# A ring of fourteen weight chunks, stripes of 1024 and transposes by VectorE in the expert stage of a decoder trunk

## The reference

```python
def swiglu(h, w1, w3, w2):
    return (jax.nn.silu(h @ w1) * (h @ w3)) @ w2

def moe_ffn(h, router_w, w1, w3, w2):      # h (256, 1024); w1, w3 (8, 1024, 3584); w2 (8, 3584, 1024)
    logits = (h @ router_w).astype(jnp.float32)
    vals, idx = lax.top_k(logits, 2)
    probs = jax.nn.softmax(vals, axis=-1)
    gate = jnp.sum(jax.nn.one_hot(idx, 8) * probs[..., None], axis=-2)
    out = jnp.zeros_like(h)
    for e in range(8):
        out = out + gate[..., e:e + 1] * swiglu(h, w1[e], w3[e], w2[e])
    return out
```

## Time and profile before

| | us |
|---|---|
| median of 3 runs (lowest, highest) | 1647.84 (1646.87, 1651.17) |
| the profiled execution, its own time | 1651.2 |
| its span, first to last instruction | 1649.4 |
| TensorE busy | 1614.8 (98%) |
| VectorE, ScalarE, GpSimd busy | 582.3, 397.8, 404.5 |
| mean granted TensorE clock | 0.99 |
| read from memory | 472 MB, 290 GB/s over the span |

### The profile page before, as it was taken

How to read it: one execution, slowest core, us unless ns; L and a number is a source line. 1 busy time by engine, 2 the same in 40 slices (tenths; PEclk the granted TensorE clock), 3 DMA queues, 4 the chain that set the end, 5 groups by cost and what they waited for, 6 DMA issues and landing times.

```text
span 1649.4 us, 46626 instructions
## 1 busy us (share of the span) xinstructions
PE 1614.8 (98%) x20940; PEld 1498.3 (91%) x20940; DVE 582.3 (35%) x784; ACT 397.8 (24%) x527; POOL 404.5 (25%) x541
## 2 busy tenths in 40 slices
PE   8999999999999999999999999999999999999998
PEld 5887888999978788899999999999999999999997
DVE  4799866466568977510000000000000000000002
ACT  4245455544454554510000000000000000000000
POOL 8856900999434523120000000000000000000100
PEclk9899999999999999999999999999999999999999
DMA  8453456556544455389999999999999999999996
GB/s 298 130 177 128 145 176 229 186 195 206 179 154 129 147 173 178 120 293 374 392 387 387 390 391 387 387 387 393 389 387 395 385 389 392 389 386 391 395 394 255
DMA packets 212094, 481.10 MB, mean 292 GB/s; under 512 B 7936, under 2 KB 32640, under 8 KB 211696
## 3 DMA queue, kind: packets, MB, share of 16 engines
q1 hardware_dynamic: 207456, 463.34, 77.4%
q0 software_dynamic: 4064, 14.95, 2.7%
q10 hardware_dynamic: 432, 0.65, 0.1%
HBM read 472.49 MB, written 6.42 MB: 290 GB/s over the span
## 4 chain that ended last, share of the span: by engine, by line
PE 67%; DVE 2%; DMA 1%; ACT 0%; issue 0%; DVEq 0%
PE ps L1336 33%; PE ps L1333 20%; PE ps L676 2%; PE ps L677 2%; PE ps L678 2%; PE ps L1364 2%; DMA raw<-moe_w 1%; PE ps L722 1%; PE ps L723 1%; PE ps L724 1%; DVE w_lo L306 1%; PE ps L912 0%; PE ps L1425 0%; PE ps L1300 0%; PE ps L1406 0%; DVE keybias L2169 0%
## 5 line engine op out<-in xcount | busy, mean ns | idle before, releaser
L1336 PE MATMUL ps<-raw,xgT 128*32 128x128 f32 x5424 | 611.6, 273 | 0.0
L1333 PE MATMUL ps<-raw,xgT 128*32 128x384 f32 x5424 | 604.2, 487 | 1.6 <-DMA raw<-moe_w 1.6
L1336 PEld LDWEIGHTS ps<-raw,xgT 128*32 128x32 f32 x5424 | 587.5, 110 | 0.0
L1336 PE MATMUL ps<-raw,hidT 128*32 128x128 f32 x2640 | 297.5, 273 | 0.0
L1333 PE MATMUL ps<-raw,hidT 128*32 128x384 f32 x2640 | 293.9, 486 | 0.0
L1336 PEld LDWEIGHTS ps<-raw,hidT 128*32 128x32 f32 x2640 | 287.5, 110 | 0.0
L306 DVE TENSOR_TENSOR w_lo<-raw,w_hi 128x2048 fp32r<-128x2048 f32 (+1 forms) x97 | 238.3, 2465 | 114.2 <-ACT w_hi L300 113.6
L2591 DVE COPY hidT<-ps 128x384 f32<-128x384 f32 x55 | 30.7, 558 | 564.1 <-PE ps L1364 564.1
L300 ACT ACTIVATE w_hi<-raw 128x2048 fp32r<-128x2048 f32 (+1 forms) x97 | 185.2, 1910 | 174.9 <-PE ps L678 83.4
L1333 PEld LDWEIGHTS ps<-raw,xgT 128*32 128x32 f32 x5424 | 215.9, 109 | 10.1 <-issue 9.8
L1886 ACT ACTIVATE sil<-ps 128x384 f32<-128x384 f32 (+1 forms) x67 | 33.9, 506 | 736.9 <-PE ps L1336 736.9
(11 more groups left out here) (417 smaller groups left out, 2253.1 us busy)
## 6 DMA issues: line engine op xcount, KB each, us to landing
raw<-moe_w SPq DMA_DIRECT2D x336, 1024.0 KB, 9.8
raw<-w_in SPq DMA_DIRECT2D x44, 1024.0 KB, 5.6
raw<-ffn_w SPq DMA_DIRECT2D x33, 1024.0 KB, 5.3
raw<-w_o SPq DMA_DIRECT2D x8, 1024.0 KB, 4.9
raw<-w_out_a SPq DMA_DIRECT2D x4, 1024.0 KB, 4.8
raw<-w_out_c SPq DMA_DIRECT2D x4, 1024.0 KB, 5.0
raw<-w_out_b SPq DMA_DIRECT2D x4, 1024.0 KB, 4.9
raw<-w_in SPq DMA_DIRECT2D x4, 904.0 KB, 4.8
```

The costliest lines, as they stand in the source:

```text
L1333: pe.matmul(ps[tile_rows(g), bank, 0:WIDE], x_of(g), w[:, 0:WIDE], start=first, stop=last, skip_group_check=True, tile_position=(0, TILE * g))
L1336: mm = pe.matmul(ps[SLOTS:P, bank, g * P:(g + 1) * P], x_of(g), w[:, WIDE:HALF], start=first and g == 0, stop=last, skip_group_check=True, ...
```

## The change

- Ring of 14 chunks. The six buffers of `raw` are joined by six over `w_hi` and `w_lo` (`ring_w`) and two over `hT_hi` and `hT_lo` (`ring_h`). The first six are loaded as before, the next six when all mixer chunks are consumed, the last two when the first gather is done.
- Stripes of 1024: an expert is now three pairs of 512 channels and one single (`HALVES = (2, 2, 2, 1)`). Banks 0 and 1 take a pair's w1 product, 2 and 3 its w3 product, 4 and 5 the down sums; SiLU and multiply work on both banks at once.
- Up chunks of a pair are two row tiles of 1024 columns (runs of 4 KB). Those of the single keep four of 512. Down chunks take rows so that partition p has four rows lying together in memory, of which a chunk takes two: runs of 8 KB, every 16 KB. The hidden channels are turned in the matching order.
- No transposes on TensorE in the first round: VectorE turns `hid_pair` and the gathered tokens in blocks of 32 by 32, from SBUF to SBUF.
- Down products are split 388 + 3 x 124 columns in place of 384 + 3 x 128.
- The loops over stripes are written out; for TensorE, VectorE, ScalarE and SP an expert is one body. The first expert's loads stand ahead of SP's loop. The four stores of the output share one semaphore.

```diff
+TOKEN_AT = HALF - 32
+Y_WIDE = WIDE + 4
+Y_REST = HALF - Y_WIDE
+PAIR = 2 * HALF
+HALVES = (2, 2, 2, 1)
+RING = 14
...
+        with ExitStack() as ring:
+            ring_w = sb("ring_w", [P, 2 * SPLIT, CHUNK], F32, ring)
...
+            w2e = moe_w2[0].rearrange("e (k p j) n -> p (e k) j n", p=P, j=4)
-            w2e = moe_w2[0].rearrange("e (k p) n -> p (e k) n", p=P)
...
+                def load_ring(m, turns, src):
+                    first = rnd == 0 and isinstance(turns, int) and turns == 0 and m - MOE0 < RING
+                    if first and m - MOE0 >= RAW + 2 * SPLIT:
+                        sp.wait_ge(S["gather_ps"], 2)
+                    if first and m - MOE0 < RAW:
+                        sp.wait_ge(used, m - RAW + 1)
+                    elif first:
+                        sp.wait_ge(used, MOE0)
+                    else:
+                        sp.wait_ge(used, value(sp, m - RING + 1 + RING * turns))
+                    sp.dma_start(ring_view(m, tuple(src.shape[1:])), src).then_inc(ring_sem(m), 16)
...
                 def up(m, turns, w, e, t):
+                    ks = 4 // HALVES[t]
+                    for c in range(KD // ks):
+                        row = value(sp, KD * e + ks * c)
+                        load_ring(m + c, turns, w[:, bass.ds(row, ks), t * PAIR:t * PAIR + HALVES[t] * HALF])
                 def down(m, turns, e, t):
+                    for c in range(2 * HALVES[t]):
+                        row = value(sp, K2 * e + 2 * t + c // 2)
+                        j = 2 * (c % 2)
+                        load_ring(m + c, turns, w2e[:, bass.ds(row, 1), j:j + 2, :].rearrange("p o j n -> p (o j) n"))
...
+                def four_tiles(bank, x_of, w, first, last, wide=WIDE):
+                    rest = HALF - wide
                     for g in range(TILES):
+                        pe.matmul(ps[tile_rows(g), bank, 0:wide], x_of(g), w[:, 0:wide], start=first, stop=last,
                                   skip_group_check=True, tile_position=(0, TILE * g))
                     for g in range(TILES):
+                        mm = pe.matmul(ps[SLOTS:P, bank, g * rest:(g + 1) * rest], x_of(g), w[:, wide:HALF],
...
-                def turn_hidden(i):
-                    pe.wait_ge(S["hid_done"], i + 1)
-                    for k in range(TILES):
-                        tr = pe.transpose(ps[:, 4, k * P:k * P + P], hid[:, k * P:k * P + P], ident[:, :])
-                    tr.then_inc(S["hidT_ps"], 1)
...
+                def turn_gathered(e, w3_used):
+                    dve.wait_ge(S["xg_loaded"], value(dve, 16 * e))
+                    dve.wait_ge(used, value(dve, w3_used))
+                    for g in range(TILES):
+                        for q in range(4):
+                            src = xg_tok[tile_rows(g), :].rearrange("s (k q n) -> s k q n", k=KD, q=4)[:, :, q, :]
+                            ins = dve.transpose(xgT[tile_rows(q), :, tile_rows(g)], src)
+                    ins.then_inc(S["xg_turned"], 1)
+
+                def turn_hidden(at, halves, free, dst=hidT):
+                    dve.wait_ge(S["hid_done"], value(dve, at))
+                    if free is not None:
+                        dve.wait_ge(used, value(dve, free))
+                    turned = dst[:, 0:4 * halves * SLOTS].rearrange("p (c s) -> p c s", s=SLOTS)
+                    for h in range(halves):
+                        for g in range(TILES):
+                            for q in range(4):
+                                rows = tile_rows(g if q < TILES else TILES)
+                                col = h * WIDE + P * (q if q < TILES else g)
+                                src = hid_pair[rows, col:col + P].rearrange("s (n j) -> s j n", j=4)
+                                ins = dve.transpose(turned[tile_rows(q), 4 * h:4 * h + 4, tile_rows(g)], src)
+                    ins.then_inc(S["hidT_made"], 1)
...
+                    stripe(i + 1, n, n + 8, 2, 2)
+                        pick_slots(value(dve, e + 1), rnd)
+                    stripe(i + 2, n + 12, n + 20, 2, 2)
+                        tokens(e + 1)
+                    stripe(i + 3, n + 24, n + 28, 2, 1)
+                        turn_gathered(e + 1, n + 28)
+                    stripe(i + 4, n + 32, n + 40, 1, 2)
...
-                pool.wait_ge(S["gather_ps"], 2 * e)
+                if e >= 2:
+                    pool.wait_ge(S["xg_turned"], e - 1)
```

More of the change, by code:

```diff
@@ L632, in expert @@
                 def expert(e, last):
[L633 to L641, removed]
@@ L649, in experts @@
+                    if not last:
+                        up(m, turns, w1e, e + 1, 0)
+                        up(m + 4, turns, w3e, e + 1, 0)
+                        m += 8
+                    down(m, turns, e, LAST)
+                up(n, 0, w1e, 0, 0)
+                up(n + 4, 0, w3e, 0, 0)
+                first = 0
+                if rnd == 0:
+                    expert(0, False)
+                    first = 1
+                with sp.Fori(first, EXPERTS - 1) as e:
                     expert(e, False)
@@ L1367, in down @@
-                def down(n, i, turns, first=False, middle=None):
-                    pe.wait_ge(S["hidT_copied"], i - DENSE_STRIPES)
-                    for chunk in range(2):
+                        for k in range(ks):
+                            kk = ks * c + k
+                            w = ring_view(m, (ks, HALF * halves))[:, k, :]
+                            for half in range(halves):
+                                mm = four_tiles(2 * which + half, lambda g: xgT[:, kk, tile_rows(g)],
+                                                w[:, half * HALF:(half + 1) * HALF], kk == 0, kk == KD - 1)
@@ L1371, in down @@
+                        mm.then_inc(used, 1)
+                def down(n, i, turns, halves, first=False):
+                    pe.wait_ge(S["hidT_made"], i - DENSE_STRIPES)
+                    for chunk in range(2 * halves):
                         m = n + chunk
                         loaded(m, turns)
+                        turned = hidT[:, chunk // 2 * WIDE:(chunk // 2 + 1) * WIDE]
                         for k in range(2):
                             for half in range(2):
-                                mm = four_tiles(2 + half, hidden_tile(hidT, 2 * chunk + k),
-                                                slot_view(raw, m, (2, D))[:, k, half * HALF:(half + 1) * HALF],
-                                                first and chunk == 0 and k == 0, False)
@@ L1470, in expert @@
                         pe.wait_ge(S["acc_done"], acc_before(rnd, e))
-                    down(n0 + 8, i + 1, turns, first=True)
-                    if last or rnd > 0:
+                    down(n + 8, i + 1, turns, 2, first=True)
+                    if pick_turned:
                         turn_pick(e)
-                    first = 2
-                    if rnd == 0 and not last:
-                        first = 3
-                        step(i + 1, turns + 1, middle=lambda: find_tokens(e + 1))
-                        down(n0 + 8, i + 2, turns + 1)
@@ L1479, in expert @@
-                    with pe.Fori(first, MOE_STRIPES - 1) as t:
-                        step(i + t - 1, turns + t - 1)
-                        down(n0 + 8, i + t, turns + t - 1)
-                    t = MOE_STRIPES - 1
-                    def next_tokens():
-                        if not last and rnd == 0:
-                            turn_gathered(e + 1)
-                        elif not last:
-                            pe.wait_ge(S["pickT_done"], scattered_before(rnd, e) + 1)
-                            gather(e + 1)
@@ L1493, in expert @@
-                    step(i + t - 1, turns + t - 1, after=next_tokens)
-                    down(n0 + 8, i + t, turns + t - 1, middle=(lambda: turn_hidden(i + t)) if last else None)
+                    n += 12
+                    step(n, i + 1, turns, 2)
+                    if not pick_turned:
+                        find_tokens(e + 1)
+                    down(n + 8, i + 2, turns, 2)
+                    n += 12
+                    step(n, i + 2, turns, 1)
+                    if not last and rnd > 0:
+                        pe.wait_ge(S["pickT_done"], scattered_before(rnd, e) + 1)
+                        gather(e + 1)
```

286 lines of the change are left out of this document (147 added, 139 removed).

## The result

The kernel after takes 1610.35 us (median; 1608.24 to 1611.76) against 1647.9 us before: ratio 0.9768 [0.9748, 0.9787], 37.5 us less. The forecast was 1602, some 46 us less. The profiled execution took 1608.24 us with a span of 1606.5; before it was 1651.2 and 1649.4.

A forecast was written before the change was run, and what follows sets the result against it. TensorE's fourth column group paced the passes, with DMA very near. TensorE's savings of 52.6 us gave 1587.4, the stream 1588 to 1594; last pass 1591, 49 us earlier, made 1602 us; range 1592 to 1624, 65% for 1596 to 1610.

The forecast's parts named there:

- TensorE's part: Expert stage: transposes gone, down split with drifting column groups, no stall; 52.6 us saved, last pass ending at 1587.4 us.
- the meeting of the two limits: End of expert stage: DMA and TensorE finishing together cost a little more than either; last pass taken at 1591 us.
- the pass-by-pass 109.8: Rival, expert passes: column groups cannot drift, each pass costs the slower, 109.83 us an expert; time 1606 to 1608; 7%.
- A regular wait of the down products for VectorE: Sign, once an expert: down products waiting on VectorE would show its transposes to be too slow.
- the transposes are too slow: Rival, VectorE: above 0.43 us each, every expert waits; 1615 us at 0.50, 1720 at 0.91; 5%.
- VectorE's part: Transposes of hidden pair and gathered tokens: 0.30 us per 128 columns, 7.1 us a pair, all hidden behind products.
- My limit of 0.43: VectorE's transposes before the half pair: hidden while one costs under 10.4 / 24 = 0.43 us.
- DMA's part: Expert weight stream: longer runs at 404 to 413 GB/s; last chunk lands at 1584 us, last pass 1588 to 1594.
- layout rival: Down chunk loads: 8 KB reads at 16 KB steps hit the same memory channels; decisive from 0.41 us more a chunk; 3%.
- DMA rival: Expert weight stream: long runs bring nothing, all chunks at 387 GB/s, last pass 1628, time 1639 us; 20%.
- the gathers as a lump: Last expert: 2 MB of gathers come as a lump, named beside the meeting limits in taking 1591 us.
- the waits come late: Sign of being right, expert stage: TensorE's waits for chunks are few and late.

The follow-up runs named there:

- r1: Kernel after with each down chunk loading only half its data, all engine work kept: 1600.98 us, 0.9739 of the kernel before.
- r2: r1 with the down products split evenly, 384 + 3 x 128 columns: 1606.52 us, 0.9772 of the kernel before.
- m2: Kernel after with VectorE's transposes reading contiguous columns, the multiply writing them in that order: 1610.97 us, 0.9786 of the kernel before.
- f3: f1 with the pairs' up chunks read in 2 KB runs: 1626.53 us, 0.9880 of the kernel before.
- f1: Kernel after with about half of the experts' products left out on TensorE, transfers untouched: 1600.61 us, 0.9727 of the kernel before.
- f2: f1 with down chunks of two rows lying end to end, 4 KB runs instead of 8 KB: 1605.17 us, 0.9756 of the kernel before.
- m4: Kernel after with the edits of m2 and m3 together: 1611.95 us, 0.9788 of the kernel before.
- s2: s1 with the later experts' indirect token gathers replaced by direct loads, 32 bytes a row after the second expert: 1602.86 us, 0.9742 of the kernel before.
- s1: Kernel after with the half pair's up chunks loaded in 4 KB runs, same bytes, half of them wrong columns: 1604.79 us, 0.9761 of the kernel before.
- m1: The kernel after run again unchanged, as reference on another chip: 1611.29 us, 0.9784 of the kernel before.
- m3: Kernel after with SP issuing a chunk only when the chunk six back has landed, ring still 14: 1609.91 us, 0.9779 of the kernel before.

## Why the prediction was right, and where it was short

**The number.** 1610.35 us lies inside the stated range, just past the upper end of the likely stretch (1596 to 1610). The total is closer than its terms. In the profiled execution the stage is 12.9 us longer than forecast (889.5 against 1591 - 714.41 = 876.6), and 6.2 us of that came back because the stage started sooner. Nothing in the prediction foresaw this; it is luck. Of the 12.9 us, 6.8 belong to TensorE's part (r1's 879.8 against 873.0) and 6.1 to the meeting of the two limits.

**TensorE's part: right in its mechanism, some 7 us short.** The L1364 and L1425 sets are gone. The up passes keep their times and the down passes go at 0.326 and 0.318 us; the column groups drift and the period is the larger sum, 108.9, not the pass-by-pass 109.8: r1 against r2 shows 0.80 of the 1.12 us, the rest going with the shorter wait for VectorE. To 108.9 come 0.43 us for the token search (I had 0.25) and 0.5 to 0.6 us of wait for VectorE (I had none): 109.94, which is r1's beat. Counted over the stage that is 8 x 109.94 - 0.43 = 879.1 us (879.8 in r1's trace) against my 873.0 (1587.4 - 714.41). A regular wait of the down products for VectorE, once an expert, was on my list of signs that the transposes are too slow; it was there, at 0.5 us.

**VectorE's part: mis-sized at 0.30 us, measured 0.42.** My limit of 0.43 was the cover of 10.4 us divided by 24. The 24 real ones fill 10.3 us, and TensorE still waits 0.5 us behind them, so the cover was thinner than the arithmetic said. What I had left out is the source step of four elements. m2 shows that this did not reach the time.

**DMA's part: right by itself.** 4 KB and 8 KB runs bring what the sum said, or more: f3 shows 25.9 us for the up chunks, f1 a rate of 406 GB/s and an end within 2 us of the prediction's 1588 (the later expectation of 1585 us in all, from higher rates, missed by 16). The 2 KB to 4 KB gap of the earlier trace rows was in the run length. For 8 KB over 4 KB I had 7 us and f2 gives 4.6. A slip without weight: the 331 chunks of the sum are those from the sixth on, not from the fifth, and one more is 2.6 us. The layout rival is refuted by f2, the DMA rival (1639) by f1.

**The step that failed** is the last term of DMA's part, "Two limits that meet cost a little more than either ... I take 1591". That meant 3 to 4 us past the stream's own 1588 and TensorE's 1587.4. Measured are 5 to 7 us over the larger limit by the ratios (0.9768 and 0.9784 against 0.9739), and 9.7 by the stages of the kernel after and r1. I had named the gathers as a lump, but only those for the last expert, and gave them no price; for the other lump, the 2 KB chunks behind 4 and 8 KB ones, I had no row. And I took the stream's rate for one number, whatever runs beside it. The same transfers go at 406 GB/s in f1 and at 401 in the kernel after. As the need is 410, the ring's lead is eaten by 2.4 to 2.8 us an expert and gone after five and a half, which is why the waits come late, as forecast, and why none of m2 to m4, which take away a wait of TensorE or shorten the queue, helps. s2 does, because it holds the rate at what TensorE needs; s1 goes part of the way. The second mis-sized term is TensorE's period, as above: the token search and the wait for VectorE.

**What stays open.** The hole and its two halves are shown, by s1 and s2. Why the engines' share falls to 0.69 to 0.75 in the first half in the kernel after and m1 to m4, and stays above 1 in f1, is not: depth of the queue is excluded (m3), the cause isn't found. TensorE's full work, its greater need for chunks in that moment and the gather's place beside the 2 KB chunks are all different in f1, and a run that moves the gather alone wasn't made. A version of the kernel with no 2 KB chunk that computes the reference would need the up weights of the half pair of one expert to be loaded with those of the next or in another split; it wasn't tried.

## What to carry to other kernels

Longer runs per partition pay when the stream is within a few per cent of the bound: 2 KB to 4 KB took 26 us off a 900 us stream here, 4 KB to 8 KB 4.6. When an edit moves two limits to the same moment, make a floor of each (half the work of the one, half the data of the other), and expect both together to cost more than the larger, here 5 to 7 us in 1600: an average rate hides the few microseconds once a period in which one of them falls short. A deep ring doesn't mend a rate that is 2% too low (401 against 410 GB/s); it only says how late the waits begin, so ask what the rate is in every phase of the period.

## What the runs showed of the hardware

- A 32-partition transpose by VectorE in fp32 took 302 ns for 128 contiguous columns (m2) and 419 when the source is read at a step of four (the kernel after); 256 contiguous columns took 435.
- SP's issue of a 1 MB transfer took 0.37 us in the median with up to six on the way (m3), but 2.1 us and up to 14.2 with about eight (the kernel after). A chunk then lands 20 us after its issue, and the time is the same (0.9784 in m1, 0.9779 in m3).
- Once an expert the stream of 4 and 8 KB packets fell from some 410 GB/s to 299 and 300 where 2 KB chunks came, and to 330 to 361 beside an indirect gather of 0.39 MB. With the 2 KB chunks gone the first became 421 and 415 (s1), with the gather gone the second 415 and 408 (s2).
- The same transfers ran at 406 GB/s in f1, with half of TensorE's matmuls and the gather at another place, and at 401 in the kernel after; which of the two makes the difference is not shown.
- The two column groups of TensorE, 388 and 3 x 124 columns in one phase and 384 and 3 x 128 in the other, run with their starts up to some 0.26 us apart without a stall (the kernel after, 1079.75 and 1080.01 us). They are paced by their sums over both phases: 108.9 us an expert, where the slower of the two in each pass would give 109.8.
